# A fused transformer block on one core: weight sums of the down projection moved from VectorE to GpSimd, the spreading matmuls moved ahead of the products, the products folded into the residual one by one

## What is computed

```python
def conv_ffn(h, w_up, conv_w, conv_b, w_down, rows, cols):
    up = depthwise_conv_grid(h @ w_up, conv_w, conv_b, rows, cols)
    gate, val = jnp.split(up, 2, axis=-1)
    return (jax.nn.silu(gate) * val) @ w_down
...
    h2 = modulate(x, g_ffn, sh2, sc2)
    x = x + ga2 * conv_ffn(h2, w_up, conv_w, conv_b, w_down, rows, GRID_W)
...
    return rms_norm(x, g_final)
```

## Time and profile before

| | us |
|---|---|
| median of 3 runs | 490.46 (490.07 to 492.64) |
| the profiled execution | 488.6 |
| its span, first to last instruction | 486.4 |
| TensorE busy | 459.5 (94%) |
| VectorE busy | 389.7 (80%) |
| ScalarE busy | 104.0 (21%) |
| GpSimd busy | 43.3 (9%) |
| weights of the ring, issue to landing (median of 33) | 4.8 |

### The profile page before, as it was taken

One profiled execution on the slowest core, in us unless ns is written; L12 is line 12 of the kernel. 1 busy time (PEld: TensorE's weight loads), 2 busy tenths in 40 slices (PEclk: granted clock), 3 DMA queues, 4 the chain that ended last, 5 costly groups with the idle time before them and its releaser, 6 DMA issues.

```text
span 486.4 us, 7769 instructions
## 1 busy us (share of the span) xinstructions
PE 459.5 (94%) x2660; PEld 351.1 (72%) x2660; DVE 389.7 (80%) x815; ACT 104.0 (21%) x195; POOL 43.3 (9%) x74
## 2 busy tenths in 40 slices
PE   3799999999999899989999999999999999879994
PEld 2444456899888788878878888888888885334463
DVE  3699999999999867951057999999999997199735
ACT  5322345043122143001062101110111012100002
POOL 0100020004030322000000011110110111000000
PEclk9999999999999999999999999999999999979998
DMA  8991499545999999844998344434433442000002
GB/s 335 424 389 40 175 331 170 195 154 97 109 307 413 394 369 408 329 170 147 411 422 327 123 169 174 146 121 166 172 120 140 171 172 86 0 0 1 0 0 86
DMA packets 21786, 96.87 MB, mean 199 GB/s; under 512 B 6464, under 2 KB 7104, under 8 KB 12928
## 3 DMA queue, kind: packets, MB, share of 16 engines
q1 hardware_dynamic: 14880, 74.70, 42.7%
q0 software_dynamic: 5488, 20.19, 13.1%
q10 hardware_dynamic: 1392, 1.63, 0.9%
HBM read 93.91 MB, written 2.59 MB: 198 GB/s over the span
## 4 chain that ended last, share of the span: by engine, by line
PE 90%; DVE 5%; issue 1%; ACT 1%; DMA 1%; DVEq 0%; ACTq 0%
PE bank L658 30%; PE bank L669 12%; PE bank L466 12%; PE bank L392 6%; PE bank L623 6%; PE bank L574 6%; PE bank L441 3%; PE bank L426 3%; PE bank L350 2%; PE bank L362 2%; PE bank L455 2%; PE bank L555 1%; PE bank L414 1%; PE bank L592 1%; DMA a_raw<-s5raw 1%
## 5 line engine op out<-in xcount | busy, mean ns | idle before, releaser
L658 PE MATMUL bank<-h_all,s_region 128*128 128x256 f32 x704 | 152.4, 379 | 0.7 <-ACT ctx_region L867 0.7
L658 PEld LDWEIGHTS bank<-h_all,s_region 128*128 128x128 f32 x704 | 133.6, 190 | 19.2 <-ACT ctx_region L867 1.1
L1332 DVE SCALAR_TENSOR_TENSOR ctx_region<-ctx_region,pk_sb 128x189 f32<-128x189 f32 (+2 forms) x352 | 127.5, 434 | 0.2 <-DVE ctx_region L1332 0.2
L466 PE MATMUL bank<-h_all,ring_region 128*128 128x256 f32 x256 | 57.9, 388 | 0.0
L466 PEld LDWEIGHTS bank<-h_all,ring_region 128*128 128x128 f32 x256 | 49.5, 194 | 7.6 <-issue 0.6
L669 PE MATMUL bank<-s_region,ring_region 128*128 128x512 f32 (+1 forms) x132 | 47.6, 521 | 0.0
L669 PEld LDWEIGHTS bank<-s_region,ring_region 128*128 128x128 f32 x132 | 25.1, 190 | 22.2 <-issue 21.0
L867 ACT ACTIVATE ctx_region<-bank 128x512 f32<-128x512 f32 x22 | 13.1, 597 | 124.6 <-PE bank L658 68.2
L916 DVE TENSOR_TENSOR s_region<-s_region,power 128x2048 f32<-128x2048 f32 (+1 forms) x16 | 38.0, 2419 | 0.1
L1247 DVE SCALAR_TENSOR_TENSOR s_region<-s_region 128x1024 f32<-128x1024 f32 x28 | 33.3, 1221 | 1.7 <-DMA s_region<-mod_w 1.2
L392 PE MATMUL bank<-h_all,ring_region 128*128 128x512 f32 x64 | 30.8, 611 | 2.0 <-ACT h_all L748 2.0
(11 more groups left out here) (204 smaller groups left out, 474.8 us busy)
## 6 DMA issues: line engine op xcount, KB each, us to landing
s_region<-up_w SPq DMA_DIRECT2D x33, 1024.0 KB, 4.8
ring_region<-ring_w SPq DMA_DIRECT2D x27, 1024.0 KB, 8.2
s_region<-mod_w POOLq DMA_DIRECT2D x28, 512.0 KB, 8.2
s_region<-early_w SPq DMA_DIRECT2D x4, 1024.0 KB, 21.5
gates<-early_w SPq DMA_DIRECT2D x2, 1024.0 KB, 12.2
s_region<-k_scratch POOLq DMA_DIRECT2D x8, 256.0 KB, 12.4
x_region<-x_t SPq DMA_DIRECT2D x1, 1024.0 KB, 5.1
ctx_region<-ctx_t SPq DMA_DIRECT2D x1, 1024.0 KB, 7.4
```

The costliest lines, as they stand in the source:

```text
L466: mx = pe.matmul(bank[5 - j % 2][:, mm * TOK:(mm + 1) * TOK], ring[:, u % RING, (mm * KD + k) * P:(mm * KD + k + 1) * P], h_x[:, k, :], st ...
L658: mx = pe.matmul(bank[s % 3][:, half * TOK:(half + 1) * TOK], up_ring[:, s, (half * KD + k) * P:(half * KD + k + 1) * P], h2[:, k, :], sta ...
L1332: dve.scalar_tensor_tensor(out=o, in0=a, scalar=cw[:, tile[half], (dy + 1) * 3 + dx + 1], in1=o, op0=ALU.mult, op1=ALU.add).then_inc(s_con ...
```

## The change

GpSimd makes t1 and b12 pair by pair (`down_weight_sums`): from tile 13 on it does one pair behind each multiplication, pair i behind tile i + 13, and pairs 9 and 10 behind the last. Its loop is written out. The two spreading matmuls run ahead of product 1, with a wait for the bank that they need, and ScalarE copies their result ahead of product 1's. VectorE makes only b11 and b21, and waits for GpSimd's last pair first. Behind the products VectorE multiplies each sum by `ga2` and adds it to the residual as it comes, so that behind product 6 five operations are left where nine were. The last reciprocal goes to ScalarE as well, which scales one of the last two parts in VectorE's place; SyncE stores the other one first.

```diff
-            for f in (1, 0):
-                sp.wait_ge(s_fin, 3 - f)
-                sp.dma_start(out[1, :, f * 512:(f + 1) * 512], x1_tok[:, 1, f, :]).then_inc(s_stored, 16)
+            sp.wait_ge(s_fin, 2)
+            sp.dma_start(out[1, :, 0:512], x1_tok[:, 1, 0, :]).then_inc(s_stored, 16)
+            sp.wait_ge(s_fin1, 1)
+            sp.dma_start(out[1, :, 512:1024], x1_tok[:, 1, 1, :]).then_inc(s_stored, 16)
             sp.wait_ge(s_stored, 16 * 3)
...
-            with pool.Fori(0, KF // 2) as i:
-                for b in range(2):
-                    pool.wait_ge(s_silu, i * 2 + (b + 1))
-                    pool.tensor_tensor(ffn_act[:, bass.ds(i * 2 + b, 1), :].rearrange("p a t -> p (a t)"), silu_sb[:, b, :],
-                                       conv[:, b, TOK:2 * TOK], ALU.mult).then_inc(s_act, 1)
+            def down_weight_sums(i):
+                pool.wait_ge(s_up[i], 16 * (UP_ROUNDS + 1))
+                pool.tensor_tensor(t1[i], w_pair[:, i, 0, 1, :], w_pair[:, i, 0, 0, :], ALU.subtract).then_inc(s_t1, 1)
+                pool.wait_ge(s_t1, i + 1)
+                pool.tensor_tensor(w_pair[:, i, 0, 1, :], w_pair[:, i, 1, 1, :], w_pair[:, i, 0, 1, :], ALU.subtract).then_inc(s_t3, 1)
+
+            for j in range(KF):
+                pool.wait_ge(s_silu, j + 1)
+                pool.tensor_tensor(ffn_act[:, j, :], silu_sb[:, j % 2, :], conv[:, j % 2, TOK:2 * TOK], ALU.mult).then_inc(s_act, 1)
+                if j >= USLOTS + 2:
+                    down_weight_sums(j - USLOTS - 2)
+            for i in range(KF - USLOTS - 2, PAIRS_D):
+                down_weight_sums(i)
...
+            pe.wait_ge(s_diag, 1)
+            pe.wait_ge(s_upsb, KF - 1)
+            for f in range(2):
+                mx = pe.matmul(bank[2 + f][:, :], ones[:, :], ga2_diag[:, 4 * f:4 * f + 4, :].rearrange("p k n -> p (k n)"), start=True, stop=True)
+            mx.then_inc(s_ga2_ps, 1)
             pe.wait_ge(s_x1tok, 4)
             product(1, lambda i: act_pair[:, i, 0, 0, :], lambda i: w_pair[:, i, 0, 0, :])
             product(2, lambda i: act_pair[:, i, 1, 0, :], lambda i: w_pair[:, i, 1, 0, :])
-            pe.wait_ge(s_diag, 1)
-            pe.wait_ge(s_upsb, KF + 1)
-            for f in range(2):
-                mx = pe.matmul(bank[2 + f][:, :], ones[:, :], ga2_diag[:, 4 * f:4 * f + 4, :].rearrange("p k n -> p (k n)"), start=True, stop=True)
-            mx.then_inc(s_ga2_ps, 1)
             pe.wait_ge(s_acomb, 1)
             product(3, lambda i: s4[:, i, :], lambda i: w_pair[:, i, 1, 1, :])
-            pe.wait_ge(s_wcomb, 1)
+            pe.wait_ge(s_t1, PAIRS_D)
             product(5, lambda i: s1[:, i, :], lambda i: t1[i])
             pe.wait_ge(s_acomb, 2)
-            pe.wait_ge(s_wcomb, 2)
+            pe.wait_ge(s_t3, PAIRS_D)
             pe.wait_ge(s_ga2, 2)
             product(7, lambda i: act_pair[:, i, 0, 1, :], lambda i: w_pair[:, i, 0, 1, :])
-            pe.wait_ge(s_wcomb, 3)
+            pe.wait_ge(s_wcomb, 1)
+            pe.wait_ge(s_upsb, KF + 1)
             product(6, lambda i: s2[:, i, :], lambda i: w_pair[:, i, 0, 0, :])
-            pe.wait_ge(s_wcomb, 4)
+            pe.wait_ge(s_wcomb, 2)
             for half in range(2):
                 product((4, 8)[half], lambda i: act_pair[:, i, 1, 1, :], lambda i: w_pair[:, i, 1, 0, :], slice(half * 256, half * 256 + 256))
...
             preload_sqrt()
+            act.wait_ge(s_ga2_ps, 1)
+            for f in range(2):
+                act.activation(ga2_bc[:, 4 * f:4 * f + 4, :], bank[2 + f][:, :].rearrange("p (k n) -> p k n", k=4), ACT.Copy).then_inc(s_ga2, 1)
             act.wait_ge(s_act, KF + 2)
             act.wait_ge(s_prod, 1)
             act.activation(sums[0], bank[PRODUCT_BANK[1]][:, :], ACT.Copy).then_inc(s_p1, 1)
-            act.wait_ge(s_ga2_ps, 1)
-            for f in range(2):
-                act.activation(ga2_bc[:, 4 * f:4 * f + 4, :], bank[2 + f][:, :].rearrange("p (k n) -> p k n", k=4), ACT.Copy).then_inc(s_ga2, 1)
 
...
+            act.wait_ge(s_rec, 1)
+            act.activation(x1_tok[:, 1, 1, :], x1_tok[:, 1, 1, :], ACT.Copy, scale=token_std[:, 1:2]).then_inc(s_fin1, 1)
...
-            for lo, hi, home in t1_parts:
-                ins = dve.tensor_tensor(home, b12[:, lo:hi], b11[:, lo:hi], ALU.subtract)
-                if hi == PAIRS_D:
-                    ins.then_inc(s_wcomb, 1)
-                else:
-                    mark(ins)
-            dve.wait_ge(s_wcomb, 1)
-            dve.tensor_tensor(b12, b22, b12, ALU.subtract).then_inc(s_wcomb, 1)
+            dve.wait_ge(s_t3, PAIRS_D)
             dve.wait_ge(s_prod, 2)
...
+            def scaled(i, f, src):
+                tt(split4(sums[i]), split4(src), ga2_row(f), ALU.mult)
+
             dve.wait_ge(s_prod, 4)
             tt(sums[2], product(5), sums[0], ALU.add)
             settle()
             tt(sums[3], product(3), sums[2], ALU.add)
+            settle()
+            scaled(3, 1, sums[3])
+            settle()
+            tt(x1_tok[:, 0, 1, :], x1_tok[:, 0, 1, :], sums[3], ALU.add)
+            dve.wait_ge(s_prod, 5)
+            tt(sums[2], product(7), sums[2], ALU.add)
+            tt(sums[0], product(7), sums[0], ALU.add)
+            settle()
+            scaled(2, 1, sums[2])
+            scaled(0, 0, sums[0])
+            settle()
+            tt(x1_tok[:, 1, 1, :], x1_tok[:, 1, 1, :], sums[2], ALU.add)
+            tt(x1_tok[:, 1, 0, :], x1_tok[:, 1, 0, :], sums[0], ALU.add)
             dve.wait_ge(s_x2, 1)
-            dve.wait_ge(s_prod, 5)
-            tt(sums[1], product(7), sums[2], ALU.add)
-            tt(sums[0], product(7), sums[0], ALU.add)
             dve.wait_ge(s_prod, 6)
-            settle()
-            for i in (3, 1, 0):
-                tt(sums[i], product(6), sums[i], ALU.add)
-            settle()
-            for i, f in ((3, 1), (1, 1), (0, 0)):
-                tt(split4(sums[i]), split4(sums[i]), ga2_row(f), ALU.mult)
-            settle()
-            dve.tensor_tensor(x1_tok[:, 0, 1, :], x1_tok[:, 0, 1, :], sums[3], ALU.add).then_inc(s_x2, 1)
+            scaled(1, 1, product(6))
+            settle()
+            dve.tensor_tensor(x1_tok[:, 0, 1, :], x1_tok[:, 0, 1, :], sums[1], ALU.add).then_inc(s_x2, 1)
             dve.tensor_tensor(x1_tok[:, 1, 1, :], x1_tok[:, 1, 1, :], sums[1], ALU.add).then_inc(s_x2, 1)
-            tt(sums[0], x1_tok[:, 1, 0, :], sums[0], ALU.add)
+            scaled(3, 0, product(6))
+            settle()
+            tt(x1_tok[:, 1, 0, :], x1_tok[:, 1, 0, :], sums[3], ALU.add)
 
             dve.wait_ge(s_sumsq, 1)
             dve.tensor_scalar(token_bias[:, 0:1], token_sum[:, 0:1], 1.0 / D, EPS, ALU.mult, ALU.add).then_inc(s_eps, 1)
+            dve.wait_ge(s_std, 4)
+            mark(dve.reciprocal(token_std[:, 0:1], token_std[:, 0:1]))
             dve.wait_ge(s_sumsq, 3)
             ts(token_bias[:, 2:3], token_sum[:, 2:3], 1.0 / D, EPS, ALU.mult, ALU.add)
-            dve.wait_ge(s_std, 4)
-            mark(dve.reciprocal(token_std[:, 0:1], token_std[:, 0:1]))
...
-                dve.tensor_tensor(x1_tok[:, 1, 0, cols], sums[0][:, cols], sums[2][:, cols], ALU.subtract).then_inc(s_x2, 1)
+                dve.tensor_tensor(x1_tok[:, 1, 0, cols], x1_tok[:, 1, 0, cols], sums[2][:, cols], ALU.subtract).then_inc(s_x2, 1)
...
-            mark(dve.reciprocal(token_std[:, 1:2], token_std[:, 1:2]))
-            settle()
-            dve.tensor_scalar(x1_tok[:, 1, 1, :], x1_tok[:, 1, 1, :], token_std[:, 1:2], None, ALU.mult).then_inc(s_fin, 1)
+            dve.wait_ge(s_dve, count[0])
+            dve.reciprocal(token_std[:, 1:2], token_std[:, 1:2]).then_inc(s_rec, 1)
+            dve.wait_ge(s_rec, 1)
             ts(x1_tok[:, 1, 0, 0:256], x1_tok[:, 1, 0, 0:256], token_std[:, 1:2], None, ALU.mult)
-            settle()
             dve.scalar_tensor_tensor(out=x1_tok[:, 1, 0, 256:512], in0=x1_tok[:, 1, 0, 256:512], scalar=token_std[:, 1:2], in1=g_bc[:, 0, 256:512],
                                      op0=ALU.mult, op1=ALU.mult).then_inc(s_fin, 1)
```

More of the change, by code:

```diff
@@ L234, in build @@
         s_diag, s_ga2_ps, s_ga2 = sem("ga2_diagonals_ready"), sem("ga2_rows_in_psum"), sem("ga2_rows_ready")
+        s_t1, s_t3 = sem("first_weight_sums_ready"), sem("third_weight_sums_ready")
         s_acomb, s_wcomb = sem("activation_sums_ready"), sem("down_weight_sums_ready")
+        s_rec, s_fin1 = sem("last_reciprocal_ready"), sem("last_scaled_by_act")
         s_p1, s_grow, s_sumsq, s_eps = sem("first_product_copied"), sem("g_row_loaded"), sem("token_squares_summed"), sem("token_bias_ready")
@@ L1364, in _ @@
                     mark(ins)
-            dve.wait_ge(s_wcomb, 3)
+            dve.wait_ge(s_wcomb, 1)
             settle()
@@ L1388, in _ @@
             tt(sums[3], product(3), sums[2], ALU.add)
+            settle()
[11 more added lines that the diff above has]
+            tt(x1_tok[:, 1, 0, :], x1_tok[:, 1, 0, :], sums[0], ALU.add)
             dve.wait_ge(s_x2, 1)
```

(20 more changed lines are left out.)

## The result

The changed kernel takes 494.74 us against 489.89 before, as medians of 8 runs each; the ratio is 1.0098, with a 95% interval of 1.0066 to 1.013. It is slower, by 4.9 us where 6.7 were forecast (497.1 us, 494 to 500 for the likeliest case, 482 to 501 in all). One of the changed kernel's 8 runs (512.23 us, mean granted clock 0.931 where the others have 0.976 to 0.980) was in a slow state, and the ratio leaves it out. The profiled execution has a span of 494.3 us against 486.4.

A forecast was written before the change was run, and what follows sets the result against it. TensorE's last 130 us were taken to bound the kernel, with idle before product 3. Product 8's end at 487.4 plus a 5.7 us tail gave a 493.1 us span, +6.7, so 497.1 us as median; range 482 to 501.

The forecast's parts named there:

- likeliest case: Whole kernel: GpSimd's subtractions hold VectorE up, 497.1 us, own range 494 to 500, chance 0.64.
- Step 1: Convolutions of tiles 14 to 21: each GpSimd subtraction takes 1.36 us and costs VectorE 1.09; VectorE ends 16.6 us late.
- Step 3: VectorE's sums s1 to s4: three GpSimd operations between them add 3.3 us; product 3 starts 8.2 us later.
- rival B: Convolutions: a fixed loss of 0.46 us per operation whatever its length, 482.4 us, 485 with the clock's fall; chance 0.14.
- rival A: Convolutions: GpSimd's sums cost VectorE nothing, TensorE runs through, span 476.9 us, time 481.0 us; chance 0.08.
- break-even: Convolutions of tiles 14 to 21: 10 us late, 0.68 us lost per operation, product 3 at 430.8, gives the old end.
- Step 2: Waits for late convolutions: up matmuls don't wait; product 1's last matmul waits 6 us for ffn_act 20, hidden.
- The 19 us: Up projection: the convolution two tiles behind the needed evacuation bears some 19 us before up matmuls wait.
- rival D: Convolutions: handing over between engines costs extra, lateness nears 19 us, up matmuls wait too: 500 to 503 us; chance 0.08.
- The clock's 2.7 us: Product 3: behind the hole it runs at 1.2 GHz, 12.12 us instead of 9.44; this stays.
- Step 4: VectorE's weight sums: t1 and b12, 12.2 us, leave VectorE but had 8 us of cover, so nothing gained.
- Step 5: End behind product 8: 1.45 us lateness and 0.40 scaling gained, 0.35 lost in stores; tail 5.66 us, was 7.16.

The follow-up runs named there:

- experiment 5: The changed kernel with each of GpSimd's 128x512 subtractions split into two of 128x256: 489.72 us, ratio 0.9982.
- experiment 7: The changed kernel with GpSimd's two subtractions of a pair replaced by copies of one weight block each: 478.77 us in a single run, 488.14 before beside it.
- experiment 1: The changed kernel with t1 and b12 back on VectorE, all else as changed: 481.36 us, ratio 0.9818.
- experiment 6: The changed kernel with GpSimd's two sums of a pair replaced by two 128x1536 memsets, which read nothing: 485.51 us, ratio 0.9846.
- experiment 8: The changed kernel with GpSimd's pairs 8 to 10 waiting for s4, the activation sum ahead of product 3: 489.78 us, ratio 0.9997.
- experiment 9: The kernel before with t1 and b12 left out altogether: 490.21 us, ratio 1.0005.
- experiment 2: The kernel before with GpSimd's sums alone, VectorE without t1 and b12, spreading matmuls and end as before: 498.81 us, ratio 1.0165.
- experiment 3: The kernel before with only the spreading matmuls, and ScalarE's copies of them, put ahead of product 1: 481.85 us, ratio 0.9844.
- experiment 4: The kernel before with the end alone: folded products, ScalarE's scaling and the order of the stores: 488.56 us, ratio 0.9972.

## Why the prediction was right

The sign and the mechanism were right. The terms of steps 1 and 3 were somewhat too large, that of the end a little too favourable.

- **Step 1, the price of an operation.** Forecast 1.36 us long and 1.09 lost. GpSimd's subtraction takes 1.27 to 1.31 us beside the convolutions, and VectorE loses 1.02 (two add 2.04 us to sixteen instructions). The estimate from the 4497 ns that the Trainium skill, GPSIMD Engine Reference, section Elementwise — side-by-side cycle accounting, gives for 2048 elements had been 1.27 and 1.00, nearer than the memsets. The lateness is 429.57 - 2.62 - 411.70 = 15.3 us, forecast 16.6. This is the largest term that was mis-sized: 1.3 us. That length decides, and not a fixed price (rival B), experiments 5 and 7 show. Experiment 1 rules out the written-out loop and the new order of TensorE, since there the same kernel without GpSimd's sums runs through; its span of 477.0 us is what rival A gave for sums that cost nothing (476.9), so the 15.3 us are theirs. The prediction's break-even of 10 us late and 0.68 us per operation does not fit its own product 3 at 430.8: with three operations ahead of s4 that takes some 11 us and 0.75. Nothing hangs on it, since 1.02 lies above both.
- **The rule behind it.** The Trainium skill, SBUF — State Buffer, section Who interferes with whom, has VectorE's instructions with two SBUF inputs collide only with GpSimd's reads, and those in a 2-port mode with any. The traces agree with the first half (experiment 6: the sixteen take 6.07 us with memsets and 6.04 without; experiment 7: 6.29 against 5.57 beside copies). The second half fits the tensor_scalars of experiment 6 (3.77 against 1.19), but no trace shows in which mode they ran.
- **Step 2, who waits.** The up matmuls did not wait; product 1 did, for ffn_act 20, by 5.4 us (6 forecast), and the clock fell behind that; both were hidden, since s4 came 3.6 us behind product 2's end. With s4 earlier (experiment 8) this cover is down to 0.5 us. The 19 us that the up matmuls were said to bear were never reached, so that part of rival D was not tested.
- **Step 3, s1 to s4.** 7.9 us from s1's start to product 3's (430.33 to 438.26), forecast 8.3. Experiment 8 takes GpSimd away and finds 5.0, so 2.9 for three operations, forecast 3.3. The clock's 2.7 us stayed, as forecast; experiments 5 and 8 show what the forecast did not say, that they hang on this hole: shorten it by 2.4 or 3.1 us and they go too.
- **Step 4** held: nothing gained (experiment 9). In the changed kernel the last sum on VectorE ends at 455.5, and product 6 starts near 469.3.
- **Step 5, the end.** 5.9 us, forecast 5.66. VectorE's lateness is gone (1.4 us), and from taking up product 8 to its last instruction it needs 2.7 us where it needed 3.2. But the span ends 3.1 us behind VectorE's last instruction (491.17) where it was 2.5 (483.93): the two stores at once cost 0.7, forecast 0.35 with a bound of 0.6. Of that, 0.4 is the second store's later issue (491.59).
- **The sum.** Product 3 starts 6.5 us later (8.2 forecast) and the tail is 1.3 shorter (1.5 forecast): +5.3 by the profiles, +4.9 by the medians, +6.7 forecast.

By the profiles, from the second round on, the parts alone are worth: GpSimd's sums +10.1, the spreading matmuls first -8.0, the end -0.8 in all and -1.3 in the tail. Their total, about +1, is 4 less than the change's +5.3. They don't add. Put first in the kernel before, the spreading matmuls take away a hole of 5.1 us and the fall of the clock. Behind late convolutions they bring product 3 only 4.1 us forward (112.58 in experiment 2, 108.45 in the changed kernel), since a hole of 3.6 us and the fall of the clock stay. Seen from the other side, GpSimd's sums cost 14.5 us once the rest of the change is in (experiment 1).

## What to carry to other kernels

An engine that is idle by the profile is not free if its instructions hold up those of a busy one: look for one instruction of the busy engine that already overlaps with one of the idle engine, and see how long it stood. The price here was the running time of each of the idle engine's instructions less about 0.3 us, so work belongs where the other engine waits anyway, and splitting an operation is no cure for the pace but shortens each single stand. Before moving work off an engine ask whether it was on the path: here t1 and b12 were not, and a reordering that cost nothing (experiment 3) held nearly all that these experiments found: 8.0 of 9.2 us.

## What was not expected of the hardware

- Holes of TensorE ahead of product 3 of 0.5, 1.0 and 1.2 us (experiments 8, 6, 5) were followed by full clock, product 3 taking 9.54 to 9.55 us; those of 3.6 to 6.2 us (after, before, experiments 4, 9 and 2) by 1.2 GHz for a stretch, product 3 taking 11.6 to 12.6 us. The hole ahead of product 1's last matmul shows the same: 1.7 us (experiment 6) left the clock full, 4.4 to 7.1 us (after, experiments 5, 8 and 2) did not. The last 2.4 us of a wait can thus cost twice their length.
- GpSimd stands for VectorE too: a subtraction of 1.26 us took 2.52 us beside a sum of 1.63 us, and that one 2.6.
- GpSimd memsets, which read nothing, held a float32 tensor_scalar on SBUF for the whole of two memsets in a row, behind the rest of a multiplication (3.44 us where the pair usually takes 0.73 to 1.19); VectorE did not get in between them.
